# Buffers of dense rounded-format products get homes with one address rest modulo 512 bytes

## What is computed

```python
# first block
proj = rms_norm(h) @ w_in                      # 1024 -> 27 tiles of 128 columns
mix  = concat(ssd_mixer(proj), rwkv7_mixer(proj)) @ w_out
h    = h + rms_norm(mix)
u    = causal_dwconv(rms_norm(h) @ ffn_w_up)   # 1024 -> 2 * 2816
h    = h + rms_norm((silu(gate) * val) @ ffn_w_down)   # gate, val = halves of u
# second block
proj = norm(h) @ w_in_2                        # 36 tiles of 128 columns, and 24 of gates
ys   = [gmlp(proj), gla(proj), topk_attention(proj)]
x    = x + gt1 * (sum_n sigmoid(gates_n) * (ys_n @ w_branch_n)) @ w_out_2
x    = x + gt2 * experts(norm(x))              # 16 experts, two of four in a chosen group per row
```

## The kernel before

| home | products | rest |
|---|---|---|
| normed_hi | high part of both projections' and feed-forward's input | 0 |
| in1 (low part), w_in1 | first projection | 112 |
| y1 hi and lo | w_out1 | 112 |
| w_out1, slots 0, 1, 2 | w_out1 | 16, 80, 112 |
| in_ff (low part), w_ff | feed-forward up, w_ff also down | 16 |
| acts hi and lo | feed-forward down | 16 |
| in2 (low part), w_in2 | second projection | 96 |
| w_br0 | branches 0 and 1, with their gates | 96 |
| w_br | branch 2 with its gates, and w_out_2 | 0 |
| ya, yb, yc, merged2, hi and lo | branches, w_out_2 | 0 |
| rows of experts' blocks 1 to 6 | experts | 0 |
| rows of experts' block 0 | experts, in fixed_data | that of fixed_data |
| expert_hi 0, 1, 2; expert_lo 0, 2 | experts | 0 |
| expert_lo 1 | experts, every third step | 96 |

## Time and profile before

### The profile page before, as it was taken

The page is one execution under the profiler, slowest core; times in us unless marked ns, Lnnn a source line. Parts: engine busy times, 40 slices in busy tenths (PEclk is TensorE's granted clock), DMA queues, the critical chain, the costliest instruction groups (busy, mean ns, idle before and its releaser), DMA issues.

```text
span 1735.5 us, 29242 instructions
## 1 busy us (share of the span) xinstructions
PE 1665.7 (96%) x11984; PEld 1289.8 (74%) x11984; DVE 1184.6 (68%) x1604; ACT 481.8 (28%) x743; POOL 678.6 (39%) x382
## 2 busy tenths in 40 slices
PE   8999988989799999999799999999999999999998
PEld 6887667767578888888578788778788767667665
DVE  7959786656488887888776179397555626666764
ACT  4122444422221011010331122221331025444452
POOL 4675000022446666666446534335445650000000
PEclk9999999999899999999999999999999999999999
DMA  6222431130242222222222212113212245889883
GB/s 253 98 97 97 167 127 52 52 124 26 97 171 89 93 97 97 97 97 97 97 74 97 85 62 74 49 49 118 94 58 89 82 185 222 343 326 350 348 330 154
DMA packets 34071, 230.55 MB, mean 133 GB/s; under 512 B 4132, under 2 KB 4388, under 8 KB 8232
## 3 DMA queue, kind: packets, MB, share of 16 engines
q1 hardware_dynamic: 30240, 214.48, 34.0%
q10 hardware_dynamic: 2136, 10.24, 1.5%
q0 software_dynamic: 1584, 4.21, 0.7%
HBM read 220.98 MB, written 9.50 MB: 133 GB/s over the span
## 4 chain that ended last, share of the span: by engine, by line
PE 83%; DVE 9%; DMA 3%; ACT 3%; issue 1%; POOL 1%; SPq 0%; DVEq 0%; POOLq 0%; ACTq 0%
PE psum L456 82%; DMA arena<-units 2%; DVE arena L1806 2%; PE psum L460 1%; ACT arena L1388 1%; DVE arena L1812 1%; DVE arena L1809 1%; DVE expert_lo L1806 1%; DVE in_lo L1806 1%; ACT expert_hi L1388 1%; DVE residual L1806 0%; DVE arena L2480 0%; DMA arena<-x 0%; DVE smalls L2475 0%; DVE tiny L1820 0%
## 5 line engine op out<-in xcount | busy, mean ns | idle before, releaser
L1388 ACT ACTIVATE arena<-psum 128x512 f32<-128x512 f32 (+3 forms) x298 | 150.4, 521 | 783.1 <-PE psum L456 722.5
L456 PE MATMUL psum<-arena 64*64 64x64 f32 (+6 forms) x2852 | 212.0, 256 | 16.5 <-DVE arena L1806 10.7
L456 PEld LDWEIGHTS psum<-arena 64*64 64x64 f32 (+4 forms) x2852 | 141.5, 143 | 72.2 <-issue 41.3
L456 PE MATMUL psum<-normed_hi,w_in_hi 128*128 128x512 f32 x488 | 193.7, 397 | 1.1 <-ACT arena L1388 0.5
L456 PE MATMUL psum<-normed_hi,w_in_lo 128*128 128x512 f32 x488 | 192.1, 394 | 0.0
L456 PE MATMUL psum<-in_lo,w_in_hi 128*128 128x512 f32 x488 | 191.3, 392 | 0.0
L1806 DVE TENSOR_TENSOR arena<-arena,psum 128x512 f32<-128x512 f32 (+2 forms) x200 | 111.8, 589 | 114.1 <-PE psum L456 80.5
L1812 DVE SCALAR_TENSOR_TENSOR arena<-arena,fixed_data 128x512 f32<-128x512 f32 x138 | 169.2, 1228 | 11.7 <-DVE arena L1809 0.2
L2733 POOL TENSOR_TENSOR w_ff_lo<-weight_ring,w_ff_hi 128x1024 fp32r<-128x1024 f32 x65 | 165.1, 2539 | 5.4
L2733 POOL TENSOR_TENSOR w_in_lo<-weight_ring,w_in_hi 128x1024 fp32r<-128x1024 f32 x61 | 155.2, 2544 | 5.1
L2731 POOL TENSOR_SCALAR w_in_hi<-weight_ring 128x1024 fp32r<-128x1024 f32 x61 | 72.3, 1185 | 176.2 <-PE psum L456 160.2
(11 more groups left out here) (288 smaller groups left out, 3573.1 us busy)
## 6 DMA issues: line engine op xcount, KB each, us to landing
weight_ring<-units SPq DMA_DIRECT2D x124, 1024.0 KB, 4.9
arena<-units SPq DMA_DIRECT2D x55, 1024.0 KB, 7.0
normed<-units SPq DMA_DIRECT2D x20, 1024.0 KB, 7.4
slots<-arena ACTq DMA_DIRECT2D x7, 516.0 KB, 8.8
arena<-slots SPq DMA_DIRECT2D x7, 516.0 KB, 5.8
fixed_data<-fixed ACTq DMA_DIRECT2D x1, 2944.0 KB, 10.3
arena<-x SPq DMA_DIRECT2D x4, 512.0 KB, 5.9
arena<-bias_rows ACTq DMA_DIRECT2D x2, 896.0 KB, 4.5
```

The lines of the kernel that those rows point to most:

```text
L456: return nc.tensor.matmul(o, l, r, start=start, stop=stop)
L1388: return nc.scalar.activation(o, i, func, **kw)
```

## The change

It alters start addresses alone; the instructions, their order, their waits and their transfers stay as they are. Multiples of P (128) are given to the homes of the dense rounded products:

- YM, the mixers' output, goes from 14,448 to 14,464, and with it WK and all that is counted from it: in1, w_in1, y1, w_out1's third slot, the mixers' work areas. w_out1's other slots go to rests 0 and 0.
- SG (a moved copy of the gate's input) and `strips` move with them.
- The feed-forward's areas are ordered anew: activations 0, accumulators 4096, convolution tiles 8192 and 10256, in_ff 20608, w_ff 24704; the first chunk's places move too.
- in2 goes from 26,080 to 25,984, w_in2 and w_br0 to 21,888, and expert_lo 1 with e_raw 1 to in2's place.
- The rows of experts' block 0 move inside fixed_data by the difference of rests between it and `residual`.
- Routing's small tiles (`late`) move from the arena, where in2's new place would cover them, to the part of fixed_data that held the attention's bucket table.

```diff
--- before.py
+++ after.py
@@ -228,7 +228,8 @@
 
 
         PROJ = 0
-        YM = N_PROJ * PADW
+        YM = 113 * P
+        assert YM >= N_PROJ * PADW
         WK = YM + 8 * T
 
         def proj(t, r0=0, r1=P, shift=0):
@@ -261,8 +262,8 @@
                 return hi[:, :], lo[:, :]
 
         y1 = MixIn("y1", KT, YM, None, WK + 6144)
-        w_out1 = Triple("w_out1", ((2064, 2064 + CHUNK), (9808, 9808 + CHUNK), (WK + 4608, WK + 10240)))
-        strips = A(30064, 64)
+        w_out1 = Triple("w_out1", ((2048, 2048 + CHUNK), (77 * P, 77 * P + CHUNK), (WK + 4608, WK + 10240)))
+        strips = A(30080, 64)
 
         s_XD, s_XS2, s_BT, s_SI, s_GT, s_HB = [
             WK + o for o in (0, 2048, 4096, 5120, -1024, 6656)]
@@ -306,16 +307,16 @@
         def chunks(ap, i):
             return ap.rearrange("p (t i c) -> p t i c", t=NT, i=2)[:, :, i, :]
         TW = PROJ + DT * PADW
-        SG = PROJ + ZZ * PADW
+        SG = 93 * P
         mod_rows = proj(ZZ + 4)[:, 0:256]
         mod_rows2 = [[A(at_ + 256 * j, 256) for j in range(2)] for at_ in (28800, 17920)]
         MOD_COLS = 256
 
-        F_UB, F_CB, F_ACC, F_ACT, F_CMB, F_IN, F_W = 0, 2064, 4112, 8208, 12304, 20496, 24592
+        F_ACT, F_ACC, F_UB, F_CB, F_CMB, F_IN, F_W = 0, 4096, 8192, 10256, 12304, 161 * P, 193 * P
         in_ff = Tiles("in_ff", KT, F_IN, x_hi)
         q_ff = 2 * 14 + KT
         q_in2 = q_ff + 6 * NF
-        w_ff = WeightsAfter("w_ff", F_W, q_ff, 8208, 13344)
+        w_ff = WeightsAfter("w_ff", F_W, q_ff, F_ACT, 105 * P)
         acts = Tiles("acts", 4, F_ACT, None, F_ACT + 2048)
         class Pair:
 
@@ -353,9 +354,10 @@
 
         sig = [[p2(t) for t in (IQ, IQ + 1, IK, MISC)], [tiny[:, 0:T], tiny[:, T:2 * T]],
                [A(DV * T + i * T) for i in range(4)]]
-        in2 = Tiles("in2", KT, n_arena - 4096, x_hi)
-        w_in2 = WeightsAfter("w_in2", n_arena - 8192, q_in2, 16896, 18432)
-        w_br = [Weights("w_br0", W2 + 3552)] * 2 + [
+        IN2 = 203 * P
+        in2 = Tiles("in2", KT, IN2, x_hi)
+        w_in2 = WeightsAfter("w_in2", IN2 - 4096, q_in2, 16896, 18432)
+        w_br = [Weights("w_br0", IN2 - 4096)] * 2 + [
             WeightsApart("w_br", W2 + 4096, AV * T, 2 * 14 + KT + 6 * NF + 2 * 18 + 4 * 6, DK * T, GR * T)]
         ys = [Tiles("ya", 4, AU * T, None, AV * T), Tiles("yb", 4, GR * T, None, AV * T),
               Tiles("yc", 4, DQ * T, None, AU * T)]
@@ -367,10 +369,10 @@
         ring_at = ring_base
         res_at = xn_at - 4 * KT * T
         e_hi = [part(f"expert_hi{i}", 0, 4096, b) for i, b in enumerate((arena_at + 4 * 14336, arena_at, res_at))]
-        e_lo = [part(f"expert_lo{i}", 0, 4096, b) for i, b in enumerate((xn_at, arena_at + 4 * 26080, arena_at + 4 * 4096))]
-        e_raw = [xn.rearrange("p a b -> p (a b)"), A(26080, 4096), A(4096, 4096)]
+        e_lo = [part(f"expert_lo{i}", 0, 4096, b) for i, b in enumerate((xn_at, arena_at + 4 * IN2, arena_at + 4 * 4096))]
+        e_raw = [xn.rearrange("p a b -> p (a b)"), A(IN2, 4096), A(4096, 4096)]
         e_down = [A(8192, UNIT), A(8192 + UNIT, UNIT), ring[:, 0, :]]
-        sel_at = C0 + CONSTS["sel16"][0]
+        sel_at = C0 + CONSTS["sel16"][0] + (res_at - fix_at) // 4 % P
         xt_at = [(sel_at, fix_at), (12288, None), (W2, None)]
         xt_hi = [part(f"rows_hi{i}", o, D, at_) for i, (o, at_) in enumerate(xt_at)]
         xt_lo = [part(f"rows_lo{i}", o + D, D, at_) for i, (o, at_) in enumerate(xt_at)]
@@ -429,12 +431,12 @@
         ids_i = small(11).bitcast(I32)
         ids = small(11)
 
-        at_small = [25656]
+        at_small = [C0 + CONSTS["bucket"][0] + P]
 
         def late(n):
             at_small[0] += n
-            assert at_small[0] <= 26080
-            return A(at_small[0] - n, n)
+            assert at_small[0] <= C0 + CONSTS["bucket"][0] + 2 * T
+            return fix[:, at_small[0] - n:at_small[0]]
 
         pre, rk, rk_m, oc = late(20), late(20), late(16), late(4)
         ov, rank, delta = [late(4) for _ in range(3)]
```

## The result

| | before | changed |
|---|---|---|
| median, us | 1743.20 (1739.18 to 1752.41, 15 runs) | 1735.09 (1727.27 to 1742.78, 15 runs) |
| profiled execution, us | 1737.35 | 1739.57 |
| its span, us | 1735.5 | 1737.6 |
| its mean granted clock | 0.991 | 0.981 |

The account below looks back on a forecast made before the run. TensorE, busy 96% of the span, was taken as the bound; savings of 3.0 + 0.7 + 7.7 + 1.5 + 1.85 + 0.85 = 15.6 us from a 1741.29 us median gave 1725.7 us, own range 1722 to 1728, wider range 1721 to 1734.

Parts of the forecast that it names:

- "half" rival: Equal homes do not suffice where the moving stream jumps between normed_hi and the low part; half the sum, 1733.5 us; 10%.
- The reading: Dense rounded 128x512 matmuls: 389 ns when all three homes share one rest modulo 128 elements, more in every mixed case.
- no change: Rival: durations come from each stage's order of work, waits and clock, not from addresses; 1741 us; 7%.
- First projection: in1 and w_in1 to rest 0: 3.7 us saved, 3.0 counted since VectorE's conversions may cover some at the stage's end.
- w_out1: Slots 0 and 1, serving 6 of 8 tiles: 144 matmuls times 5 ns, 0.7 us saved, all on the path.
- Second projection: in2 and w_in2: 36 tiles, 864 matmuls times 1.7 ns, 1.5 us saved.
- Branches: Gates of the branches, ya and yb: 2.15 us saved, 1.85 counted, as VectorE's top-k search covers part of branch 0's gain.
- Feed-forward up: Up products of the feed-forward: 44 tiles, 1,056 matmuls times 7.3 ns, 7.7 us saved, all counted.
- with 346 us left both still fit: Feed-forward: VectorE's 290.99 us and GpSimd's 222.86 us of work fit the shortened stage, so all 7.7 us counts.
- Experts: Expert steps, slot 1 1.3 us and three other steps 0.4; half counted, 0.85 us, as weight transfers share the chain.
- Moved without a price: Mixers' areas, SG, feed-forward accumulators and convolution tiles, routing's small tiles: 0 us, bound 7.8 us either way at the very most.
- slower rival: Mixers' small full-precision products pay for WK's move by 16 elements; 5.5 ns each would give 1747 us; 5%.

Follow-up runs that it names:

- the small kernel: A separate kernel computing nothing of the reference, 21 groups of 48 rounded 128x512 matmuls at varied rests; 226.7 ns start to start at weights' rests 0 and 64, 233.3 or 233.4 at 16.
- the kernel with the mixers back: Changed kernel with the mixers' areas back at 14,448 and 18,544, in1, w_in1 and convolution tiles kept at rest 0; 1731.26 us beside the changed kernel's 1730.78.

## Why the prediction was right, and where not

Forecast: 1725.7 us, faster, range 1721 to 1734. It was faster; the median of 1735.09 us lies 1.1 us above the range, and the mean of all 40 runs, 1733.2, at its upper end. Counted from the base that the forecast used, the ratio of 0.9942 gives 1731.2, inside the range. That it is inside is partly luck: the forecast's own range was 1722 to 1728, and what lies between 1728 and 1734 was there for the "half" rival. The size is that of the "half" rival (1733.5), its mechanism is not. Point by point:

- **The reading** (389 ns is the state that equal homes settle into, whatever the stage): right. All groups are at 389, and the small kernel shows that the address alone does it. The rivals "half of it" and "no change" fall: even with the moving stream jumping between normed_hi and the low part all three products read 389. Moving the weights alone by 16 elements costs 6.7 ns on 226.7. The rules of the Trainium skill ("SBUF — State Buffer", sections "Who interferes with whom" and "Door 1: The DMA port swizzle"), by which TensorE never waits for anyone in its two reads, and which name no part of an address but its 16-byte line, don't account for this; here the measurement decides.
- **First projection**, 3.0 of 3.7: measured 3.3 at equal clock (154.33 and 151.00 us, both with 3.4 us at 1.2 GHz). **w_out1**, 0.7: 0.4 in the mean of the traces (60.2 us in four with mixed homes, 59.7 in eight with equal ones). **Second projection**, 1.5: 1.3. **Branches**, 1.85: 1.8, of which branch 0 gave 0.95, so its search on VectorE covered nothing and other parts gave less.
- **Feed-forward up**, 7.7: right as a saving of TensorE, wrong as a saving of time in most of the traces. Without the first wait, and with half of the time at 1.2 GHz taken off, the stage takes 362.8 us (three traces) against 370.7 (three): 7.9. But five of the six executions with all these homes at 0 and the order unchanged had the wait, 2.85 us, and all paid 1.6 us for the clock. The step that failed is "with 346 us left both still fit". It set 291 us of VectorE's work against the whole stage. VectorE's slack is in the later passes: from 536 to 780 us of the kernel before it waits for TensorE 4.0 to 6.6 us in each stretch of 40 to 42 us. In the first one, 496 to 536 us, it waited for TensorE for 1.3 us in all, ahead of its sums of the down products:

```profile
L1806 DVE TENSOR_TENSOR arena<-arena,psum 128x512 f32<-128x512 f32 x8 | 5.3, 684 | 1.5 <-PE psum L456 1.3
```

  "TensorE beginning to wait on VectorE" was named as what would shrink the term, and did.
- **Experts**, 0.85: nothing. Step products are at 389, but the stage took 271.2 to 272.8 us in the changed kernel's four traces and 269.8 and 272.3 in the two of the kernel before. The one of 269.8 us had no time at 1.2 GHz in this stage, the other five had 3.4 us. The gain forecast is smaller than the spread between executions, and none of it is seen. The forecast gave half to the weight transfers. In the first trace of the changed kernel the chain that ended last has six of them (start us, us):

```profile
1471.78 10.69 DMA arena<-units
1530.58 10.59 DMA arena<-units
1570.79 10.07 DMA arena<-units
1590.65 11.58 DMA arena<-units
1650.70 9.79 DMA arena<-units
1690.45 10.00 DMA arena<-units
```

  They add up to 62.7 us, where the kernel before had four, with that of the earlier trace rows 42.9 us. But the repeats don't bear this out: the changed kernel's have three, five and four transfers there (31.4, 52.6 and 41.1 us), and the second trace of the kernel before four (40.4 us). So it is not shown that what TensorE saved went to the transfers. The term "half" was mis-sized; why is open.
- **Moved without a price**: right, by the mixers at low 1.2 GHz time (226.95 against 225.39 us with 3.4 and 0 us at 1.2 GHz) and by the kernel with the mixers back. The slower rival falls.
- **The clock** had no term. The forecast took the clock of the two kernels as equal; at equal clock the change is worth 14.7 us of the 15.6 forecast. The lower clock costs 3.0 us in the mean over all runs, 2.0 where both ran side by side.
- **The base.** 1741.29 was a median of three; over 15 runs it is 1743.20, 1.9 us more. Three runs within 0.8 us of each other are no measure of a kernel whose times spread over 13 us.

From 15.6: the wait in five of six executions 2.4, the clock at the feed-forward's end 1.6, experts 0.85, w_out1 and the second projection 0.5, less 0.3 for the first projection and 0.2 for the feed-forward's size: 10.8 us left. The ratio gave about 10, all runs 11.7. The part of the clock that is not explained, 1.4 us, would make it 9.4; the uncertainty of either number is about 2.

At equal clock the account is less closed. The parts without the 1.6 us of clock leave 12.4 us, the runs say 14.7. One reading would close it. The three executions of the changed kernel whose traces have the wait stand, brought to a clock of 0.985 with 1.45 us for each 0.001, at 1733.8, 1735.6 and 1735.6 us, the one without it at 1729.3, and all 40 at 1731.3 in the mean. So most runs may have been without the wait, which would put the parts at 14.8. No trace exists of those runs; this is not shown.

What stays open: why the clock falls at the feed-forward's end with equal homes. TensorE did the same before it in both kernels, an unbroken run of products and then an idle 2.54 or 2.55 us. Nothing tried took this away with equal homes in the feed-forward, and no experiment separated the pace of the products from the moment at which the stage ends. What decides the time at 1.2 GHz in the mixers is open too.

## What to carry to other kernels

When matmuls of one form, without idle time, differ by a per cent or two in their mean duration, lay the durations beside the addresses of both operands: for rounded products give weights and moving operand one rest modulo 256 bytes (64 float32 elements), which a kernel of matmuls alone, like the one above, can confirm. Before counting such a saving in full, look for VectorE's slack in the pass that has least of it, not in the stage's sum. With times that spread more than the effect, compare at equal clock over many runs, and trust a feature of a trace only after the same program has shown it again: here the wait of 2.85 us was present in three executions of the changed kernel and absent in the fourth, and six transfers in the chain of one execution were three, five and four in the others.

## What was not expected of the hardware

- The pace of a rounded 128x512 matmul depends on where its weights lie against its moving operand: 226.7 ns at an equal rest modulo 256 bytes, 228.8 at 48, 232.4 at 32, up to 233.4 at 8 or 16 elements, and 234.3 to 234.5 in the feed-forward's pattern. The runs show no such thing in the 64x64 full-precision products (221 and 222 ns with either home).
- VectorE and GpSimd in each other's way: a VectorE operation of 0.75 us lasts up to 2.77 us beside a GpSimd instruction, and between executions of the same program a phase later by 0.1 to 0.3 us goes with the absence of a 2.85 us wait 45 us on.
- The mean granted clock of one program varies from 0.976 to 0.989 between executions (the changed kernel; before 0.980 to 0.991), and 0.001 goes with 1.4 to 1.5 us.
